# Two means of squares: six of eight tiles summed by GpSimd first, then 24 small matmuls instead of 64, one block later

## The reference, cut to what matters

```python
def rmsnorm(x, g):
    xf = x.astype(jnp.float32)
    y = xf * lax.rsqrt(jnp.mean(xf * xf, axis=-1, keepdims=True) + EPS)
    return (y * g.astype(jnp.float32)).astype(x.dtype)

x = x + rmsnorm(merged @ w_o[l], norm_mix_post[l])
h = rmsnorm(x, norm_mlp_pre[l])                      # touched
f = jnp.square(jax.nn.relu(h @ w_up[l])) @ w_down[l]
x = x + rmsnorm(f, norm_mlp_post[l])
# second block
h = rmsnorm_2(x, norm_mix[layer])                    # touched
proj = h @ w_in[layer]
```

## Time and profile before

| | us |
|---|---|
| median of 3 runs | 1439.07 (1438.96 to 1439.25) |
| the profiled execution | 1442.82 |
| its span, first to last instruction | 1441.0 |
| PE busy | 1419.8 (99%) |
| VectorE busy | 787.0 (55%) |
| ScalarE busy | 538.3 (37%) |
| GpSimd busy | 173.9 (12%) |

### The profile page before, as it was taken

The page is one execution under the profiler, slowest core; times in us unless marked ns, Lnnn a source line. Parts: engine busy times, 40 slices in busy tenths (PEclk is TensorE's granted clock), DMA queues, the critical chain, the costliest instruction groups (busy, mean ns, idle before and its releaser), DMA issues.

```text
span 1441.0 us, 17906 instructions
## 1 busy us (share of the span) xinstructions
PE 1419.8 (99%) x7475; PEld 1164.4 (81%) x7475; DVE 787.0 (55%) x1059; ACT 538.3 (37%) x767; POOL 173.9 (12%) x145
## 2 busy tenths in 40 slices
PE   7999999999999999999999999999999999999998
PEld 5888788988888888887888776778878888888887
DVE  6998673754234343377584665564535554434433
ACT  6232344643332241255543436662333222212214
POOL 1030013100000000110231712111210000000002
PEclk9999999999999999999999999999999999999999
DMA  6322224113323223313234212112332233233221
GB/s 195 115 88 89 87 88 148 58 59 107 98 88 115 91 88 110 109 60 117 68 87 117 71 60 59 31 30 59 103 102 89 88 99 106 88 104 101 88 87 59
DMA packets 134880, 129.92 MB, mean 90 GB/s; under 512 B 14688, under 2 KB 130288, under 8 KB 134768
## 3 DMA queue, kind: packets, MB, share of 16 engines
q1 hardware_dynamic: 133664, 125.11, 28.1%
q0 software_dynamic: 992, 3.47, 0.8%
q10 hardware_dynamic: 144, 0.20, 0.0%
HBM read 126.27 MB, written 2.10 MB: 89 GB/s over the span
## 4 chain that ended last, share of the span: by engine, by line
PE 96%; DVE 1%; ACT 1%; DMA 1%; POOL 0%; issue 0%; SPq 0%; ACTq 0%; DVEq 0%
PE gemm L459 73%; PE gemm L567 3%; PE gemm L944 3%; PE misc L971 2%; PE misc L990 1%; PE misc L793 1%; PE gemm L651 1%; PE misc L598 1%; PE gemm L598 1%; DMA w_raw<-in_w_in 1%; PE gemm L728 1%; PE gemm L1064 1%; PE gemm L886 1%; PE gemm L960 1%; PE gemm L672 1%; PE misc L960 0%
## 5 line engine op out<-in xcount | busy, mean ns | idle before, releaser
L1666 DVE TENSOR_TENSOR w_lo<-w_raw,w_hi 128x2048 fp32r<-128x2048 f32 (+1 forms) x108 | 245.8, 2276 | 178.5 <-ACT w_hi L1127 178.3
L459 PE MATMUL gemm<-h_hi,w_hi 128*128 128x512 f32 x828 | 325.2, 393 | 1.8 <-ACT gate_tanh L1381 1.8
L459 PE MATMUL gemm<-h_hi,w_lo 128*128 128x512 f32 x828 | 322.4, 389 | 0.0
L459 PE MATMUL gemm<-h_lo,w_hi 128*128 128x512 f32 x828 | 322.3, 389 | 0.0
L1127 ACT ACTIVATE w_hi<-w_raw 128x2048 fp32r<-128x2048 f32 (+1 forms) x113 | 213.8, 1892 | 143.9 <-PE gemm L459 139.5
L459 PEld LDWEIGHTS gemm<-h_hi,w_hi 128*128 128x128 f32 x828 | 155.5, 188 | 37.4 <-issue 4.6
L459 PEld LDWEIGHTS gemm<-h_hi,w_lo 128*128 128x128 f32 x828 | 155.4, 188 | 32.8
L459 PEld LDWEIGHTS gemm<-h_lo,w_hi 128*128 128x128 f32 x828 | 155.5, 188 | 32.1 <-issue 0.5
L459 PE MATMUL gemm<-n_hi,w_hi 128*128 128x512 f32 x336 | 130.9, 390 | 0.0
L459 PE MATMUL gemm<-n_lo,w_hi 128*128 128x512 f32 x336 | 130.7, 389 | 0.0
L459 PE MATMUL gemm<-n_hi,w_lo 128*128 128x512 f32 x336 | 130.7, 389 | 0.0
(11 more groups left out here) (470 smaller groups left out, 1997.6 us busy)
## 6 DMA issues: line engine op xcount, KB each, us to landing
w_raw<-in_w_in SPq DMA_DIRECT2D x62, 512.0 KB, 4.6
w_raw<-in_w_down SPq DMA_DIRECT2D x32, 512.0 KB, 4.1
w_raw<-in_w_up SPq DMA_DIRECT2D x28, 512.0 KB, 4.4
w_raw<-in_w_ffn_gate SPq DMA_DIRECT2D x22, 512.0 KB, 4.5
w_raw<-in_w_ffn_up SPq DMA_DIRECT2D x22, 512.0 KB, 4.5
w_raw<-in_w_ffn_down SPq DMA_DIRECT2D x16, 512.0 KB, 4.5
w_raw<-in_w_o SPq DMA_DIRECT2D x8, 512.0 KB, 4.0
w_raw<-in_w_out SPq DMA_DIRECT2D x8, 512.0 KB, 4.1
```

Of the source, the lines that this page charges most:

```text
L459: mm = nc.tensor.matmul(bank[:], w(s)[:, kt, col0:col0 + P], x(n), start=first, stop=last)
L1666: V.tensor_tensor(part(lo_of(s), s), part(raw_of(s), s), f(part(hi_of(s), s)), SUB).then_inc(S("lo_done"), SLABS_AT[s])
```

## The change

The mean of squares at both places is computed in another way and at another point of PE's order. GpSimd adds the squares of tiles 0 to 5 into `SQA` (five additions, each waiting for the next square and for the addition before). PE then calls `mean_rows` three times, for `SQA` and for tiles 6 and 7: 12 instructions a place instead of 32. It does so after the first block of low halves, and not ahead of it; the spread of 1/rms moves from ahead of the second block to ahead of the third. The additions stand in GpSimd's queue behind `add_squares(0)` and `add_squares(1)`, ahead of the table loads. `SQA` may be overwritten once the mean of the layer's output is done, which `mean_ready` tells.

```diff
+        def x_mean(n):
+            pe.wait_ge(S("x_sq_added"), 5 * n + 5)
+            mean_rows(SQA[:], True, False)
+            pe.wait_ge(S("x1_squared"), KT * n + KT)
+            mean_rows(Y[:, 6, :], False, False)
+            mean_rows(Y[:, 7, :], False, True).then_inc(S("mean_ready"), 1)
...
         def first_up():
...
-            for k in range(KT):
-                pe.wait_ge(S("x1_squared"), k + 1)
-                mm = mean_rows(Y[:, k, :], k == 0, k == KT - 1)
-            mm.then_inc(S("mean_ready"), 1)
             for b in range(4):
                 if b == 1:
+                    x_mean(0)
+                if b == 2:
                     spread_rstd(M[2], 2)
...
         def first_in():
...
-            for k in range(KT):
-                pe.wait_ge(S("x1_squared"), KT + k + 1)
-                mm = mean_rows(Y[:, k, :], k == 0, k == KT - 1)
-            mm.then_inc(S("mean_ready"), 1)
             for n, (s, c0, m) in enumerate(blocks):
                 if n == 1:
+                    x_mean(1)
+                if n == 2:
                     spread_rstd(M[2], 4)
...
+        def add_x_squares(n):
+            pool.wait_ge(S("mean_ready"), 2 + 2 * n)
+            for k in range(1, 6):
+                pool.wait_ge(S("x1_squared"), KT * n + k + 1)
+                if k > 1:
+                    pool.wait_ge(S("x_sq_added"), 5 * n + k - 1)
+                Q.tensor_tensor(SQA[:], SQA[:] if k > 1 else Y[:, 0, :], Y[:, k, :], ADD).then_inc(S("x_sq_added"), 1)
+
         add_squares(0, 1, lambda j: (S("wo_squared"), j + 1))
+        add_x_squares(0)
         add_squares(1, 3, lambda j: (S("ysq_ready"), j + 1))
+        add_x_squares(1)
```

## The result

| | before | after |
|---|---|---|
| median of the comparison | 1439.25 us (1438.96 to 1440.95, 5 runs) | 1447.17 us (1445.86 to 1449.09, 5 runs) |
| profiled execution | 1442.82 | 1449.09 |
| its span | 1441.0 | 1447.3 |

The ratio is 1.005, with a 95% interval of 1.0039 to 1.006: the change makes the kernel slower by 7.9 us. I had predicted +2.7 and a range that ended at 1445.2, so the direction was right and the size was not.

What follows compares the result with a forecast made beforehand. PE, busy 99% of the span, was taken as the bound; 0.35 (MLP) + 2.1 (attention) + 0.2 (slab stall) = +2.7 us took the profiled 1442.82 to 1445.5, less 3.75 for timed runs: 1441.8, range 1436.6 to 1445.2.

Steps and rivals of the forecast that it cites:

- Sum 3.6 us: At each place, VectorE's loss to GpSimd's five additions: 3 x 0.67 plus 2 x 0.81, bounded by nothing and 4.1.
- My overlay: Additions laid over VectorE's run at the attention place: first three meet x_T additions, last two meet low halves; MLP the same.
- over 8: Sign of being right: VectorE's low halves at both places take over 8 us instead of 5.39.
- My 6.5: By the skill's rule, VectorE loses 1.30 per addition, up to 6.5 us a place, with the end near 1447.
- The stall of 0.2 for the weight slab: Behind the attention place, slab low halves ready at 678.1 but PE wants them at 677.9: 0.2 us stall.
- The clock: Rival, chance 0.20: starved PE's clock falls at the attention place, costing 1.5 to 3 us more; 1443.3 to 1444.8.
- The saving on PE: Mean of 12 instead of 32 instructions saves PE 1.18 us per place, 2.36 in all.
- The cast's gain: Ahead of the attention place, GpSimd's cast leaves 630.3, ending its collision with VectorE's x_T addition: everything 0.67 us earlier.
- ScalarE's high halves: At both places they come up to 0.9 us later, which is covered.
- The later point: Spread one block later: 4.0 us later at attention, giving a 0.2 stall; 2.3 later at MLP, costing zero.
- Hidden: Rival, chance 0.18: VectorE loses nothing to the additions at either place; time 1436.7.
- half of the collisions: Rival, chance 0.10: x_T additions slip between, only low halves pay, 1.6 us a place; time near 1438.0.

Runs made afterwards that it cites:

- filler: The changed kernel with an unused-result matmul ahead of each low matmul of the first block, so PE works while waiting: 1445.89 us against 1440.82 before, ratio 1.0047.
- attn_only: The change made at the attention place alone, the MLP place keeping the old mean: 1445.73 us, ratio 1.003 to the kernel before.
- mlp_only: The change made at the MLP place alone, the attention place keeping the old mean: 1442.55 us, ratio 1.0015 to the kernel before.
- adds_only: Kernel before plus GpSimd's five additions a place, sum unused; old 32-instruction mean at its old point, spread waiting for the last addition: 1443.94 us against 1440.66, ratio 1.0024.
- three_tiles: Kernel before with GpSimd's table cast later and GpSimd adding only tiles 0 to 2 at the MLP place (24 mean instructions): 1440.36 us against 1440.75, ratio 1.0.
- write_only: The changed kernel with each GpSimd addition replaced by two memsets, which read nothing (sum wrong): 1438.4 us against 1440.82 before, ratio 0.9986.
- moved_only: Kernel before with its 32-instruction mean and the spread one block later, no GpSimd additions: 1440.65 us against 1440.66, ratio 0.9996.

## Why the prediction was wrong

**The step that failed: "Sum 3.6 us", VectorE's loss a place.** In the profile after, the MLP place loses 0.80 + 1.06 + 1.81 + 1.03 = 4.7 (two x_T additions, the pair, the low halves) and the attention place 0.80 + 0.70 + 1.77 + 1.01 = 4.3. I had taken 0.67 and 0.81 as the price of a meeting, and five times 0.81, 4.1, as the most that it could be. A meeting has no fixed price. VectorE loses what is left of GpSimd's instruction when it starts: in the earlier trace rows the x_T addition started 0.23 into a cast of 1.04 us and lost 0.67. In the kernel after, VectorE starts 0.06 to 0.46 into additions of 1.29 or 1.30 and loses 0.70 to 1.11, or 0.94 on average over five at the MLP place. The prediction said that the rows "show less than the whole" and took this for a partial wait; it was a whole wait for the remainder.

My overlay was also off. The delays keep VectorE and GpSimd in step, so four x_T additions were hit and one low half, not three and two; the low halves take 6.42, not the "over 8" that I named as a sign of being right (and that my own two meetings, 5.39 + 2 x 0.81 = 7.0, did not give either). At full clock and measured from the last high matmul (MLP, filler) and from the right spread (attention, attn_only), the eighth low half is 4.68 and 4.28 us later than before: 1.08 and 0.68 above my 3.6.

The Trainium skill's rule, SBUF — State Buffer, section "Who interferes with whom", that the second to issue is blocked until the first has finished, is what these rows show. My 6.5 from it took VectorE to start together with GpSimd each time. That it gave an end "near 1447", and the median is 1447.17, is luck: at full clock the change costs 5.05 us and not the 8 behind that figure.

**Small terms behind it.** I let the mean start 0.25 us after the last low half; a matmul that has just waited takes 0.50, and the mean starts 0.49 after it. The mean takes 0.80 instead of 0.71, and what follows it 0.11 more than before. That is 0.44 a place. Together, MLP 0.35 + 1.08 + 0.44 = 1.87 against 1.83 measured; attention, without the cast's gain, 2.77 + 0.68 + 0.44 = 3.89 against 3.88. The stall of 0.2 for the weight slab did not come (*next* is 11.06 in attn_only and filler). So the change costs 5.05 us at full clock, where I had 2.7.

**The clock came on top, not instead.** I had made it a rival at 0.20, at the attention place alone. In the profile after it fell in both places and took 9.84 - 5.07 = 4.8 us there: 1.6 at the MLP place, 1.6 in *attn*, and 1.6 in *next*, in the fall behind the four matmuls on 16 rows. Over the timed runs it is less: (1 - granted clock) x span has a mean of 4.6 us in the five runs of after and of 3.1, 3.3 and 2.5 in 31, 23 and 16 runs of before, so about 1.5 more (the clock is given to 0.001, 1.4 us, and after's five values scatter by 2.6 about their mean, so this is rough and might be nothing). attn_only has 5.8 and mlp_only 4.3, adds_only 2.2 and filler 3.2, and adds_only has few of PE's tile-by-tile waits (one at the MLP place, where mlp_only has several), which speaks for these waits as the cause. It is not shown: three_tiles, without such waits, has 3.7 (against 2.5 in its runs of before) and a fall in its profile, and attn_only's profile has the waits and no fall. What sets off a fall in one execution stays open.

**The rest of the 7.9.** 5.05 + 1.5 is 6.5. Before's median in the comparison with after was 1439.25 (5 runs), but 1440.66, 1440.82 and 1440.75 in the larger sets. Against these, after's 1447.17 is 6.4 to 6.5 slower. The last 1.4 us is thus how low the five runs of before lay. Whether this is the draw of five, or both kernels were faster in that comparison, the runs don't tell.

**What held.** The saving on PE (write_only, 1.11 of 1.18). The cast's gain: 0.67 predicted, and 0.66 to 0.67 in every kernel in which it came later (*norm* 14.06 or 14.07). In moved_only and mlp_only, where it stayed near 630, *norm* is 14.81 and 14.43. ScalarE's high halves: I had them up to 0.9 late; the last is later by 1.53 (right spread to last high matmul, 9.70 to 11.23), PE waited 1.6 us for four of them, and this was covered as argued, since the low halves ended later still. The later point: free in the MLP place, 0.7 at the attention place, in moved_only. "Hidden" and "half of the collisions" fell.

## What to carry to other kernels

- Handing elementwise sums to an idle GpSimd is not free while VectorE works on two SBUF operands: for each GpSimd instruction that reads SBUF, count as lost what is left of it when VectorE's operation comes (near 0.9 us for an addition of 128x512 here), and lay it on whoever waits for VectorE. A loss read off one meeting is no unit price: read where in the other instruction it began. Take work off PE only as long as VectorE's slack covers that (two additions did, five did not).
- Small work that stands in front of a late operand is cover. Once it goes, the wait takes its place, and the clock may fall as well.

## What the runs showed that I had not expected

- The clock can fall while PE counts as busy throughout (three_tiles, 652 to 656, 0.70 and 0.50). The Trainium skill, TensorE: Matmul & The Clock Gate, section "HAM oscillation — how this bites in real kernels", tells of falls where PE waits between bursts of matmuls; the fall of mlp_only comes behind waits too, though these are 0.17 us at most, and that of three_tiles does not. Executions of one kernel differ: before spreads over 1438.5 to 1446.5 us in 31 runs.
- In write_only GpSimd's cast took 3.07 us beside VectorE's weight low halves (2.23, unchanged), and 1.30 in the kernel after: there it was GpSimd that paid. Its cast started 0.05 behind VectorE's operation, while in every meeting above it was VectorE that started second.
